# Last normalisation of a decoder step: gains multiplied in by GpSimd from ScalarE's copies, with an early square-root table and two idle matrix products

## The reference, cut to what matters

```python
h = layernorm(ALPHA * x + m @ w_o, ln1_g, ln1_b)
return layernorm(ALPHA * h + hier_moe(h, ...), ln2_g, ln2_b)

def layernorm(x, g, b):
    mu = mean(x); var = mean((x - mu) ** 2)
    return (x - mu) * rsqrt(var + LN_EPS) * g + b

def hier_moe(x, ...):            # gate: 2 experts of one group per token
    for e in range(32):
        hu = x @ w_up[e]         # 1024 -> 512
        h = silu(hu[:, :256]) * hu[:, 256:]
        y = y + gate[:, e:e+1] * (h @ w_down[e])
```

## Time and profile before

| | |
|---|---|
| Median of 3 executions | 571.61 us (571.46 to 576.95) |
| The profiled execution | 572.16 us, of it 570.3 us span |
| Mean granted TensorE clock | 0.97 |
| TensorE busy | 527.6 us (92% of the span) |
| VectorE, ScalarE, GpSimd busy | 266.6, 107.7 and 48.2 us |
| Transfers | 162.47 MB, 285 GB/s over the span |
| Chain that ended last | PE 64%, transfers 14%, VectorE 13% |

### The profile page before, as it was taken

One profiled execution on the slowest core, in us unless ns is written; L12 is line 12 of the kernel. 1 busy time (PEld: TensorE's weight loads), 2 busy tenths in 40 slices (PEclk: granted clock), 3 DMA queues, 4 the chain that ended last, 5 costly groups with the idle time before them and its releaser, 6 DMA issues.

```text
span 570.3 us, 9541 instructions
## 1 busy us (share of the span) xinstructions
PE 527.6 (92%) x3941; PEld 321.3 (56%) x3941; DVE 266.6 (47%) x791; ACT 107.7 (19%) x253; POOL 48.2 (8%) x64
## 2 busy tenths in 40 slices
PE   8999999998999999999999998999999795948894
PEld 4555456474577778887776557555655251512332
DVE  1272753898889976864652696411002000100016
ACT  1001112011323534322000331111111010100123
POOL 0000000001011435320000000000000000002000
PEclk9999999999999999999999998999999897989987
DMA  8990442944293568744889957799999999999972
GB/s 299 401 347 8 147 148 63 383 151 151 76 332 111 186 213 285 240 163 155 347 342 411 311 183 296 257 431 419 426 423 430 419 427 421 431 421 421 402 239 79
DMA packets 48338, 162.47 MB, mean 285 GB/s; under 512 B 6274, under 2 KB 25180, under 8 KB 39076
## 3 DMA queue, kind: packets, MB, share of 16 engines
q1 hardware_dynamic: 39472, 138.76, 62.8%
q0 software_dynamic: 3728, 14.33, 7.2%
q10 hardware_dynamic: 5092, 8.74, 4.5%
HBM read 159.02 MB, written 2.77 MB: 284 GB/s over the span
## 4 chain that ended last, share of the span: by engine, by line
PE 64%; DMA 14%; DVE 13%; ACTq 5%; issue 2%; ACT 1%; SPq 0%; POOLq 0%; POOL 0%; DVEq 0%
PE bank L654 14%; PE bank L833 13%; DMA ring<-in_w_up 13%; PE bank L1218 7%; PE bank L601 4%; PE bank L1248 3%; PE bank L1364 2%; ACTq L1665 2%; ACTq L1664 2%; PE bank L1188 2%; PE bank L1170 2%; DVE ring L1889 2%; DVE gates L2022 2%; PE bank L670 2%; PE bank L1287 1%
## 5 line engine op out<-in xcount | busy, mean ns | idle before, releaser
L654 PE MATMUL bank<-ring,work 128*128 128x512 f32 (+2 forms) x224 | 92.1, 547 | 0.1
L833 PE MATMUL bank<-work,ring 128*128 128x264 f32 x384 | 90.1, 390 | 0.0
L833 PEld LDWEIGHTS bank<-work,ring 128*128 128x128 f32 x384 | 71.4, 190 | 14.5 <-issue 2.5
L1218 PE MATMUL bank<-ring,work 128*32 128x512 f32 x304 | 59.0, 654 | 8.8 <-DMA proj<-in_w_up 7.6
L654 PEld LDWEIGHTS bank<-ring,work 128*128 128x128 f32 x224 | 39.5, 190 | 28.8 <-issue 25.1
L2552 DVE SCALAR_TENSOR_TENSOR work<-work,bank 128x256 f32<-128x256 f32 x8 | 3.4, 422 | 86.7 <-ACT work L1725 86.7
L1218 PE MATMUL bank<-proj,work 128*32 128x512 f32 x96 | 40.1, 646 | 4.1 <-DMA ring<-in_w_up 4.1
L2564 DVE COPY gates<-bank 128x512 f32<-128x512 f32 x7 | 4.8, 691 | 64.3 <-PE bank L1364 56.2
L1218 PEld LDWEIGHTS bank<-ring,work 128*32 128x32 f32 x304 | 15.9, 119 | 32.6 <-issue 32.5
L976 PE MATMUL bank<-work,ring 128*128 128x264 f32 x128 | 31.4, 391 | 0.7 <-ACT gates L1570 0.6
L976 PEld LDWEIGHTS bank<-work,ring 128*128 128x128 f32 x128 | 23.4, 190 | 8.7 <-issue 3.4
(11 more groups left out here) (366 smaller groups left out, 822.9 us busy)
## 6 DMA issues: line engine op xcount, KB each, us to landing
ring<-in_w_up SPq DMA_DIRECT2D x19, 2048.0 KB, 19.8
ring<-in_w_in SPq DMA_DIRECT2D x21, 1024.0 KB, 6.7
ring<-in_w_down SPq DMA_DIRECT2D x8, 2048.0 KB, 20.2
proj<-in_w_up SPq DMA_DIRECT2D x5, 2048.0 KB, 22.5
extra<-in_w_up SPq DMA_DIRECT2D x4, 2048.0 KB, 26.4
proj<-in_w_down SPq DMA_DIRECT2D x3, 2048.0 KB, 27.0
ring<-in_w_o SPq DMA_DIRECT2D x4, 1024.0 KB, 10.1
misc<-in_w_up SPq DMA_DIRECT2D x3, 1024.0 KB, 22.4
```

What stands on the lines that cost most here:

```text
L654: last = mm(bank[2 * (i % 2) + t][:, 0:w], lhs[:, k, 128 * t:128 * t + 128], rhs[:, k % 4, :], start=(k == 0), stop=(k == KT - 1))
L833: last = mm(b[:, 0:TOK], w[:, k, 128 * (n % 2):128 * (n % 2) + 128], xT[:, k, 0:TOK], start=(k == 0), stop=(k == KT - 1))
L1218: last = mm(bank[5][32 * j:32 * j + 32, :], xTe[q // 2 % 2][:, k, s0:s0 + CAP], up_at(q, j, k), start=(k == 0), stop=(k == KT - 1))
```

## The change

Four edits, and what follows from them.

1. **Idle products.** In the router stage TensorE forms one more identity product into bank7, ahead of its wait for `r_ready` 4, and in `gains` one into bank5, ahead of the first gains product. Their results aren't used.
2. **Table ahead.** ScalarE takes a square root of one column behind the two negations and ahead of `down_out(6)`, so that the square-root table is loaded there. (A second such line stands in the branch that isn't entered.)
3. **Gains by GpSimd.** The products y*g of VectorE, but for the first, go to GpSimd: ScalarE copies y of a part from its bank into `y3` (`x_copied`), and GpSimd multiplies it in place by `gbc` (`z_ready` for the first, `y_scaled` for the other two). VectorE signals its sums to ScalarE by `var_ready`, whose counts move. TensorE waits for both first parts ahead of its two identity products, and not for each.
4. **Signals.** Each of the four two-row products counts `fin_ps`; the readers wait for their own count. VectorE forms the samples' reciprocal and bias ahead of `y_out(0, 6)`.

```diff
@@ tensor, router stage
             wo_second(1, (4, 5, 6)).then_inc(wo_ps, 1)
+            mm(bank[7][:, :], ident, h3[:, 0, 0:512], start=True, stop=True)
             pe.wait_ge(r_ready, 4)
@@ tensor, gains()
                 pe.wait_ge(ht2_sb, QUADS)
+                mm(bank[5][:, :], ident, h3[:, 0, 0:512], start=True, stop=True)
                 for dh in range(2):
@@ tensor, end
+            pe.wait_ge(z_ready, 2)
             for t in range(2):
-                pe.wait_ge(z_ready, t + 1)
                 mm(bank[5 + 2 * t][:, :], ident, y3[:, t, 0:512], start=True, stop=False)
...
             for i, (b, first) in enumerate(((5, False), (6, True), (7, False), (0, True))):
-                last = mm(bank[b][:, :], turned_c[32 * i:32 * i + 2, :], lnrows[32 * i:32 * i + 2, :], start=first, stop=True)
-            last.then_inc(fin_ps, 1)
+                mm(bank[b][:, :], turned_c[32 * i:32 * i + 2, :], lnrows[32 * i:32 * i + 2, :], start=first, stop=True)\
+                    .then_inc(fin_ps, 1)
@@ scalar
                 act.activation(lnrows[p0:p0 + 1, :], lnrows[p0:p0 + 1, :], ACT.Copy, scale=-1.0).then_inc(gb_sb, 1)
+            act.activation(th[:, 0:1], ident[:, 0:1], ACT.Sqrt)
             down_out(QUADS - 2)
...
-            for t in range(2):
-                act.wait_ge(var_ready, 4 + t)
+            def x_copy(part):
+                act.activation(y3[:, :, y_cols(part)], bank[2 * part - 1][:, :].rearrange("p (t n) -> p t n", t=2),
+                               ACT.Copy).then_inc(x_copied, 1)
+            def y_std(t):
                 std_ = turn_me[:, 64 * t + 1:64 * t + 2]
                 act.activation(std_, std_, ACT.Sqrt, bias=eps_col).then_inc(std_ready, 1)
+            act.wait_ge(var_ready, 4)
+            act.activation(y3[:, 1, 0:512], y_part(1, 0), ACT.Copy).then_inc(x_copied, 1)
+            act.wait_ge(var_ready, 5)
+            x_copy(1)
+            act.wait_ge(var_ready, 6)
+            y_std(0)
+            act.wait_ge(var_ready, 7)
+            x_copy(2)
+            act.wait_ge(var_ready, 8)
+            y_std(1)
...
-            act.wait_ge(fin_ps, 1)
             for t, b in ((0, 5), (1, 7)):
+                act.wait_ge(fin_ps, 2 * t + 1)
@@ gpsimd
+            pool.wait_ge(gb_sb, 4)
+            pool.wait_ge(x_copied, 1)
+            pool.tensor_tensor(y3[:, 1, 0:512], y3[:, 1, 0:512], gbc[:, 0:512], ALU.mult).then_inc(z_ready, 1)
+            for part in range(1, 3):
+                pool.wait_ge(x_copied, 1 + part)
+                y_ = y3[:, :, y_cols(part)]
+                pool.tensor_tensor(y_, y_, gbc[:, y_cols(part)].unsqueeze(1).broadcast_to([128, 2, 256]), ALU.mult)\
+                    .then_inc(y_scaled, 1)
@@ vector
             for t in range(2):
                 y_sums(t, 2)
                 y_var(t)
-            y_first(1)
             for t in range(2):
                 y_rstd(t)
...
-            y_scaled(1)
             dve.wait_ge(q_ps, 1)
...
-            y_scaled(2)
-            y_out(0, 6)
             dve.wait_ge(std_ready, 6)
             link(V.reciprocal(stats[:, 42:43], stats[:, 42:43]))
             link(V.scalar_tensor_tensor(stats[:, 55:56], mean_s, -1.0, stats[:, 42:43], ALU.mult, ALU.mult), n1_ready)
+            dve.wait_ge(y_scaled, 2)
+            y_out(0, 6)
             y_out(1, 0)
```

More of the change, by code:

```diff
@@ L2623, in y_sums @@
                 dve.wait_ge(comb, QUADS + (t if part == 0 else 1 + part))
-                for i in range(2 if part == 0 else 1):
+                parts = 2 if part == 0 else 1
+                for i in range(parts):
                     at = 6 * i if part == 0 else 6 + 6 * part
-                    link(V.bn_stats(y_stats[t][:, at:at + 6], y_part(t, part)[:, 256 * i:256 * i + 256]))
-            def y_scaled(part):
-                w2 = bank[2 * part - 1][:, :].rearrange("p (t n) -> p t n", t=2)
-                g2 = gbc[:, y_cols(part)].unsqueeze(1).broadcast_to([128, 2, 256])
-                tt(y3[:, :, y_cols(part)], w2, g2, ALU.mult)
+                    link(V.bn_stats(y_stats[t][:, at:at + 6], y_part(t, part)[:, 256 * i:256 * i + 256]),
+                         var_ready if t and i == parts - 1 else dchain)
             def y_var(t):
@@ L2649, in _ @@
             link(V.memset(eps_col, EPS))
-            def y_first(t):
-                tt(y3[:, t, 0:512], y_part(t, 0), gbc[:, 0:512], ALU.mult, z_ready)
             dve.wait_ge(gb_sb, 4)
             y_sums(0, 0)
-            y_first(0)
+            tt(y3[:, 0, 0:512], y_part(0, 0), gbc[:, 0:512], ALU.mult, z_ready)
             y_sums(1, 0)
```

11 lines of the change are left out of this document (8 added, 3 removed).

## The result

The changed kernel took 577.06 us (median of 20 runs, 572.54 to 583.23), the kernel before 571.78 in the same session (20 runs, 569.95 to 579.47). The medians lie 5.3 us apart. The ratio, formed without the one execution of each kernel that lay over 1.5% above its fastest, is that of the means (576.68 and 572.77): 1.0068, 95% interval [1.0041, 1.0096], so 3.9 us slower, by 2.3 to 5.5. I had forecast 572.1 with a range up to 574.3. The profiled execution took 577.48 us, its span 575.7.

The account below looks back on a forecast made before the run. Bound by weight transfers, then TensorE's own work, then a ladder of short steps between engines: 572.16 - 0.77 (router) + 1.6 (stage) - 0.9 (ladder) = 572.1 us, range 570.8 to 574.3.

Parts of the forecast that it names:

- The ladder: Last combine to the samples' normalisation, short steps between VectorE, ScalarE and TensorE; forecast 0.9 us shorter.
- are then done at 561.17 in place of 561.65: Last layernorm: VectorE's reciprocals and small products end 0.48 us earlier, since GpSimd takes over a gains product.
- VectorE and GpSimd block each other: Rival in the ladder: VectorE's two-SBUF-input products wait for GpSimd's running product; +1.45 us, 573.6 us; chance 0.27.
- GpSimd's last two steps and the transfer follow as before: Kernel's end, behind the samples' normalisation: final GpSimd steps and output transfer keep their length, no added time.
- TensorE's two identity products ... run from 559.8, so the second begins near 560.9: Last layernorm: identity products wait for GpSimd's first product, yet the second begins where it began before.
- it fits into the idle time and costs nothing: Router: the 1.12 us idle product is covered by TensorE's 1.21 us idle time.
- The stage: Quad 7's tanh on ScalarE to the last combine on TensorE; idle product and table load forecast to cost +1.6 us.
- 2.3 - 0.7 = 1.6: Stage: TensorE's products start 2.3 us later waiting for y_act of quad 6; 0.7 regained if low clock falls into the wait.
- my rival of a new drop: Stage: low clock falls on the products behind TensorE's new wait; 1.4 to 1.7 us more; chance 0.15.
- The router's 0.77: Router: idle product holds the clock, removing VectorE's 0.77 us wait; stream and TensorE move earlier, carrying to the end.
- My fifth case: Router: first idle product doesn't hold the clock or there was no drop to undo; +0.77 us, 572.9; chance 0.08.
- The table load: ScalarE ahead of down_out(6): load takes 1.28 us with no drain behind, 1.49 with the one-column square root.

Follow-up runs that it names:

- e9: Changed kernel without the idle product in the router; 574.25 us, ratio 1.0024 of the kernel before.
- e5: Changed kernel with table load between the last two down_out, no idle product at the gains, small VectorE products reading one tile; 573.96 us beside 573.05 of before.
- e11: Changed kernel without either idle product, table load between the last two down_out; stage 22.08 us, ladder 9.69 us.
- e2: Changed kernel without the idle product at the gains; its stage took 22.26 us.
- e4: Kernel before with only the router's idle product added; ratio 1.0004 of the kernel before.
- e10: Kernel before with only the idle product at the gains and the table load ahead of the last two down_out; ratio 1.0016 of before.
- e7: As e5 with one more 16-column product in the router; 572.90 us beside 573.05 of before.
- e13: Changed kernel with its router idle product 16 columns wide in place of 512; ratio 1.0061 of the kernel before.
- e14: Changed kernel run again without an edit; ratio 1.0038 of the kernel before.
- e8: Kernel before with only the samples' reciprocal and bias ahead of y_out(0); span end 34.40 us from the stage's start against 34.31 before.
- e12: As e6, also without the idle product in the router; 571.49 us against 572.02 of before, ratio 0.9980.
- e3: Changed kernel with VectorE's three small products written with one tile and per-partition scalars; its ladder took 10.92 us.
- e6: As e5, with TensorE waiting for each of the two identity products by itself again; 572.43 us beside 573.05 of before.

## Why the prediction was wrong

**The ladder had the wrong sign: the step "are then done at 561.17 in place of 561.65" priced VectorE's small products as if nothing ran beside them.** I had forecast their end 0.48 us earlier; behind the last combine it came at 5.85 (566.03 in the changed kernel, and in e9) where before had 5.17, so 0.68 later. The steps themselves were right: without the blocking and the gap, e5 took 8.52, which is 0.87 under before where I had summed 0.9. But the two `y_rstd` products waited for GpSimd. That was my rival "VectorE and GpSimd block each other", given 0.27 and +0.56 against before in the ladder; with the blocking and no gap the ladder measured +0.08 (e9), +0.30 (e11) and +0.49 (e2), that is 0.95 to 1.36 over e5, where I had priced 1.45. The blocking itself is e9's 0.95; in e11 and e2 a low clock lay over the two-row products too (1.38 and 1.56 us in place of 1.14). I had let the absence of a row against it stand as evidence, where no row of before had the two engines at work side by side. The Trainium skill, "SBUF — State Buffer", section "Who interferes with whom", states it as an exclusive lock on a shared port pair, through which VectorE reads its second SBUF input. With that rule the trace agrees, down to 128x1 operands: 0.73 and 0.99 us against 0.21 with one tile.

**The end was taken as unchanged.** "GpSimd's last two steps and the transfer follow as before" missed 0.31 us: the span ended 2.30 us behind the first issue of the samples' transfers in before, e4 and e10, and 2.59 to 2.62 behind it in all twelve kernels with the changed tail, though the last data packets ended 1.52 to 1.56 behind it in all of these. What waits there isn't shown.

**No case of mine had the gap.** "TensorE's two identity products ... run from 559.8, so the second begins near 560.9" took TensorE's issue as free. The idle products lengthen its program, and the gap then fell among the identity products. At the full clock it is worth 1.30 where nothing else is late (e5 to e7), nothing beside blocked products, and 1.2 to 1.9 where a low clock follows it (10.69 and 11.37 against 9.47). So the step "it fits into the idle time and costs nothing", on the router's product, missed a cost: with it gone the changed kernel stood at 1.0024 (e9) and with it at 1.0038 to 1.0068. These intervals overlap; the gap itself, in e7 and e13, doesn't hang on them.

**The stage was right in mechanism and in size at a like clock.** I had 2.3 - 0.7 = 1.6. Measured: 2.43 at the full clock on both sides, and 1.47 in e9, e10 and e14 against before, whose products behind the wait took 2.70 in place of 1.98. The low clock that I had put into the wait lay on the products ahead of it (e9, e14) or was absent (e10). The changed kernel's 3.20 holds 1.73 of a low clock that went on over the products (3.72 us in place of 1.98): my rival of a new drop, 1.4 to 1.7, which I had given 0.15. I had read it as something that the new idle time would set off; e11 has the same long drop without that idle time, so it comes without it as well. How often it comes with it and without it, one profile of each kernel can't tell. I had counted on one profile where the place of the low clock changes from run to run.

**The router's 0.77 didn't reach the end.** The drop that the product was to undo was there in before and e9, and in four others without the product (e8, e10, e11, e12) it was absent; in the ten profiled executions with the product it was absent too, though in three of them (e3, e6, e14) it came right behind that stretch. Where it is absent the stretch is 0.98 us shorter (8.76 against 9.74). In the changed kernel the stage began at 536.53, against 536.03 before, in spite of it. Over all profiles the stage began at 538.2 on the mean with the product (ten, 535.7 to 542.1) and at 535.7 without (six, 534.3 to 536.8). But most of that difference is there ahead of what the product could save: L601's four records behind the wait began at 348.5 on the mean with it and at 346.4 without (348.94 in the changed kernel, 346.75 before), with the same program ahead of the product, and four of the six profiles without it come from one chip. The time of e4 (1.0004, up to 1.0029) shows no loss. So the 0.98 us is there against a like start, and it is lost in the spread between executions; why the starts differ stays open. My fifth case, the product idle in vain, was the nearest to it.

**The table load** took 1.28 with no drain behind it, as the earlier trace rows said. Of the 1.38 us more that the Trainium skill, "ScalarE: Activation LUTs", section "What ACT_TABLE_LOAD costs", gives for a drain the trace shows nothing. **The single signals** were priced at nothing, and all eight records lie within 1.19 us; no run had them alone. **The reciprocal ahead** gave its 0.45 to the normalisation (0.55 in e8), but the end of e8's span didn't come earlier.

**The sum again.** At a like clock, e14's profile: to the end +1.84 over before (36.15 - 34.31), of it 1.47 of the stage, 0.08 of the ladder and 0.3 of the end; its ratio says +2.2 us. With the low clock behind the gap and over the products, the changed kernel: +4.81 (3.20, 1.30 and 0.31), its ratio +3.9. I can't say how often each comes; the two sets of runs of this one kernel gave 1.0068 and 1.0038, and their intervals overlap.

## What to carry to other kernels

When work moves to GpSimd, list the VectorE instructions that will run beside it and read two SBUF tiles, narrow ones as well: on this chain of short steps each waited until the running GpSimd instruction ended, and writing it with one tile and per-partition scalars took the wait away. An instruction added to fill an idle engine isn't free because it fits into the idle time: here it moved the place of an issue gap 200 us later onto a chain of dependent steps. Read the place of a low clock from several executions before pricing an edit that means to move it.

## What the runs showed of the hardware

- A gap of 0.9 to 1.4 us in TensorE's issue sat at a place of the program that moved with the number of products ahead of it, whatever their width (512 or 16 columns); a 16 KB instruction transfer started 2.2 to 2.9 us and ended 1.2 to 1.5 us ahead of the gap's end.
- VectorE's 128x1 product took 0.73 and 0.99 us beside a GpSimd product when both inputs were tiles, 0.21 when one was a tile and the others scalars per partition.
- In two profiles of the one changed kernel TensorE was at 1.2 GHz over the products behind the wait (3.72 us) and only over those ahead of it (the ones behind it then took 1.99 us).
- GpSimd multiplied 128x512 elements in 1.27 us, two such in 2.48.
- The span ended 2.30 us behind the issue of the last output transfers in one order of the tail, 2.6 in another and 2.95 in a third, while the last data packets ended 1.52 to 1.72 behind it.
